# Stick-breaking attention: the softplus tile split in two on VectorE, its product with the triangle of minus ones in two reduced passes

## What is computed

```python
def stick_breaking(q, k, v):
    def block(args):
        q_blk, b_idx = args
        z = jnp.einsum('bqhd,bkhd->bhqk', q_blk, k).astype(jnp.float32) * scale
        q_pos = b_idx * SB_BLOCK + jnp.arange(SB_BLOCK)
        mask = key_pos[None, :] < q_pos[:, None]
        log_1mb = jnp.where(mask, jax.nn.log_sigmoid(-z), 0.0)
        after = lax.cumsum(log_1mb, axis=3, reverse=True) - log_1mb
        w = jnp.where(mask, jnp.exp(jax.nn.log_sigmoid(z) + after), 0.0)
        return jnp.einsum('bhqk,bkhd->bqhd', w.astype(v.dtype), v)
```

## Time and profile before

| | before |
|---|---|
| median of 3 runs | 3941.0 us |
| the 3 runs | 3942.57, 3941.0, 3927.64 us |
| span of the profiled execution | 3942.1 us (its time is not listed apart from the runs; the nearest run is 3942.57) |
| TensorE busy over the span | 93% |
| VectorE, ScalarE, GpSimd busy | 51%, 42%, 3% |
| stick-breaking stage, from the first L1342 to the last L1325 | 422.4 to 569.8 us, 147 us |

### The profile page before, as it was taken

One profiled execution on the slowest core, in us unless ns is written; L12 is line 12 of the kernel. 1 busy time (PEld: TensorE's weight loads), 2 busy tenths in 40 slices (PEclk: granted clock), 3 DMA queues, 4 the chain that ended last, 5 costly groups with the idle time before them and its releaser, 6 DMA issues. The chain is left out here.

```text
span 3942.1 us, 48364 instructions
## 1 busy us (share of the span) xinstructions
PE 3658.2 (93%) x18930; PEld 2963.7 (75%) x18930; DVE 2019.1 (51%) x3935; ACT 1663.9 (42%) x3110; POOL 107.9 (3%) x119
## 2 busy tenths in 40 slices
PE   7999889999997999999897999999879999999799
PEld 6888558778876777777776777777768788888686
DVE  3144442453345777776335455555555456666542
ACT  3222561444442444443125444444433466665420
POOL 0011220000000000000000000000000000000000
PEclk9999999989997889899999999999979999999799
DMA  4343412113222212122311110011132121110311
GB/s 143 115 134 105 141 45 89 54 64 107 96 72 83 57 44 54 51 57 65 123 43 58 28 33 28 28 28 30 35 108 75 49 65 43 38 38 17 137 61 43
DMA packets 219274, 264.57 MB, mean 67 GB/s; under 512 B 62636, under 2 KB 142628, under 8 KB 218024
## 3 DMA queue, kind: packets, MB, share of 16 engines
q1 hardware_dynamic: 219048, 261.48, 20.4%
HBM read 191.43 MB, written 69.99 MB: 66 GB/s over the span
## 5 line engine op out<-in xcount | busy, mean ns | idle before, releaser
L329 PE MATMUL bank<-wh,XH 128*128 128x512 f32 x1344 | 553.5, 412 | 23.3 <-DVE wl L313 18.2
L329 PE MATMUL bank<-wh,XL 128*128 128x512 f32 x1344 | 528.4, 393 | 0.0
L329 PE MATMUL bank<-wl,XH 128*128 128x512 f32 x1344 | 528.4, 393 | 0.0
L2600 PE MATMUL bank<-XH,wh 128*128 128x512 f32 x1040 | 426.2, 410 | 27.7 <-DVE wl L2589 26.1
L2600 PE MATMUL bank<-XH,wl 128*128 128x512 f32 x1040 | 410.5, 395 | 0.0
L2600 PE MATMUL bank<-XL,wh 128*128 128x512 f32 x1040 | 409.7, 394 | 0.0
L329 PEld LDWEIGHTS bank<-wh,XH 128*128 128x128 f32 x1344 | 255.8, 190 | 86.2 <-issue 18.2
L329 PEld LDWEIGHTS bank<-wh,XL 128*128 128x128 f32 x1344 | 256.0, 190 | 60.1 <-issue 10.0
L329 PEld LDWEIGHTS bank<-wl,XH 128*128 128x128 f32 x1344 | 255.4, 190 | 55.5
L329 PE MATMUL bank<-XH,wh 128*128 128x512 f32 x704 | 281.4, 400 | 7.9 <-DVE XL L1552 7.9
L313 DVE TENSOR_TENSOR wl<-raw,wh 128x1024 fp32r<-128x1024 f32 x128 | 157.3, 1239 | 250.6 <-ACT wh L304 249.3
(11 more groups left out here) (412 smaller groups left out, 7043.9 us busy)
## 6 DMA issues: line engine op xcount, KB each, us to landing
sc_zt<-stage SPq DMA_DIRECT2D x88, 256.0 KB, 2.0
raw<-in_att_w_in SPq DMA_DIRECT2D x33, 512.0 KB, 4.2
raw<-in_even_w_in SPq DMA_DIRECT2D x32, 512.0 KB, 5.3
raw<-in_odd_w_in SPq DMA_DIRECT2D x32, 512.0 KB, 4.7
raw<-in_rec_w_in SPq DMA_DIRECT2D x32, 512.0 KB, 4.0
sc_h<-H SPq DMA_DIRECT2D x24, 512.0 KB, 2.6
sc_z<-stage SPq DMA_DIRECT2D x40, 256.0 KB, 2.0
z<-sc_z SPq DMA_DIRECT2D x8, 1024.0 KB, 5.5
```

Of the source, the lines that this page charges most:

```text
L329: done = e.matmul(out, lhsT, rhs, start=k == 0 and j == 0, stop=k == NK - 1 and j == 2)
L2600: done = e.matmul(bank[:, :], x[:, k, :], y[:, k, ts], start=k == 0 and j == 0, stop=k == NK - 1 and j == 2)
```

## The change

The softplus tile is split on VectorE in two float32r tiles: `sph`, a cast of `sp` (which rounds it), and `spr`, the rest `sp` minus `sph`. The triangle gets a float32r copy `tri`, made once (minus one is exact in it). TensorE's product with the triangle becomes two float32r matmuls, tri times sph and tri times spr, in place of the full-precision one. The product with `nones`, the products for z and with v, and GpSimd's add (which still reads `sp`) stay.

```diff
+        self.tri = c.right("tri", [P, P], R32)
+        self.sph, self.spr = (c.sbs(n, [P, 512], 4, R32) for n in ("sph", "spr"))
...
             elif what == "sum":
-                e.wait_ge(*self.plus.at(h, half, kb))
-                e.matmul(bank[:, 0:n], self.ntri[:, :], self.spl[h][:, 0:n], start=False, stop=False, skip_group_check=True)
+                if kb == 7 and h == 0:
+                    e.wait_ge(*self.whole.at())
+                e.wait_ge(*self.rest.at(h, half, kb))
+                for s in (self.sph, self.spr):
+                    e.matmul(bank[:, 0:n], self.tri[:, :], s[h][:, 0:n], start=False, stop=False, skip_group_check=True)
...
         e.wait_ge(*self.tables.at("after"))
+        e.tensor_copy(self.tri[:, :], self.ntri[:, :]).then_inc(*self.whole.up())
...
                 done.then_inc(*self.plus.up(h, half, kb))
+                e.wait_ge(*self.plus.at(h, half, kb))
+                e.tensor_copy(self.sph[h][:, 0:n], s[:, 0:n]).then_inc(*self.halved.up(h, half, kb))
+                e.wait_ge(*self.halved.at(h, half, kb))
+                e.tensor_tensor(self.spr[h][:, 0:n], s[:, 0:n], f32(self.sph[h][:, 0:n]), ALU.subtract) \
+                    .then_inc(*self.rest.up(h, half, kb))
...
-    nc = _bacc.Bacc("TRN2", target_bir_lowering=False, num_devices=1)
+    nc = _bacc.Bacc("TRN2", target_bir_lowering=False, num_devices=1, dynamic_dma_scratch_size=1024)
```

More of the change, by code:

```diff
@@ L1276, in __init__ @@
         self.run = c.flag("po")
+        self.whole, self.halved, self.rest = (c.flag("ve") for _ in range(3))
         self.marks = [[(self.kepl, (h,)) for h in range(4)] + [(self.low, (h, s // 4)) for h in range(4)] for s in range(NS)]
```

## The result

The changed kernel takes 3957.39 us in the median of 14 runs, the kernel before 3941.09 us in the median of 14. The ratio is 1.0034, 95% interval 1.0022 to 1.0046, so 9 to 18 us slower (the two medians by themselves are 16.3 us apart, inside that interval). The forecast was 3941 with a range to 3950. The half per cent that was named as the bound of a difference isn't reached, but the time is outside the range, and the change is a loss. The stage, too, is outside what the prediction allowed ("longer by over 6" was its sign of being wrong).

The account below looks back on a forecast made before the run. TensorE was taken to bound the wide slots, waits the others. Gains of 6.4 us (wide slots) and 1.2 (last sums) cancelled against added waits and switches, sum 0.0: 3941 us, own range 3936 to 3946, with rivals 3927 to 3950.

Parts of the forecast that it names:

- longer by over 6: Sign of being wrong: the changed stage, forecast at 147 us within 5, comes out more than 6 us longer.
- The price of a pass and the wide slots: Full-width triangle product 0.46 us for 0.86; 16 wide slots hide VectorE's new work and win 6.4 us.
- switches between kinds of product: TensorE changing between full-precision and float32r matmuls: 0.04 us for each of 24 full-width products, +1 us.
- The mechanism in the masked slots: New VectorE work delays the mask of w that TensorE's weigh awaits: +2.0 (384 columns), +1.1 and +0.4 us (slots 4-7, 0-3).
- The loop of two slots: Masked slots: new work, mask of w and weigh set two slots' minimum length, 5.2 us with 384 columns.
- the sum above has no term for it: Port shared by VectorE and GpSimd: in wide slots the add ends at 3.7 us, when the cast begins; no cost.
- Rival 2: Shared port takes the wide slots' gain too: 3944 to 3947 us, 3950 with masked slots worse; chance 0.17.
- The cover of 2 us: Wide slots: split ends at 4.9 us, the triangle product needing it stands at 6.9 us, so VectorE's work is hidden.
- Where half 1 is mixed: Closed chain through masks, gate product and ScalarE: 0.57 us of 128-column split in each of four slots, +2.3 us.
- The last four sums: End of the stage: no begin beside them, TensorE is the bound again, a gain of 1.2 us.
- The ceiling: Gain if TensorE were the bound everywhere in the stage: 14.4 us, 0.37% of the time.
- Rival 3: Granted TensorE clock stays at 1.2 GHz through slots 4 to 11 and 36 to 43: +23 us, 3964 us; chance 0.04.

Follow-up runs that it names:

- e4_noadd: Changed kernel with GpSimd's running sum cut to one column of each item; stage 150.9 us, ratio to the kernel before 1.0014.
- e8_order_noadd: Changed kernel with the split moved behind the mask of w and GpSimd's running sum cut to one column; stage 139.3 us, ratio to before 0.9989.
- e6_kept: Changed kernel with the four retention splits moved from slots 12, 15, 18, 21 to wide slots 22, 24, 26, 28; stage 157.2 us, ratio 1.0028.
- e11_end: Changed kernel with the split at its slot's end, behind gate product and XL, and retention splits in wide slots; stage 140.8 us, ratio to before 0.9981.
- e12_halves: Changed kernel with the split at its slot's end and retention splits in 512-column halves within slots 18 to 28; stage 139.2 us, ratio to before 0.9983.
- e2_passes: Changed kernel without the split: softplus written as float32r once and read by both passes; stage 137.0 us, ratio to the kernel before 0.9974.
- e1_order: Changed kernel with cast and subtraction moved behind the mask of w of the item two slots older; stage 146.6 us, ratio to before 1.0002.
- e5_noadd_before: Kernel before the change with GpSimd's running sum cut to one column; stage 145.7 us, one run of 3951.43 us.

## Why the prediction was wrong

- **The price of a pass and the wide slots: right.** 0.46 for 0.86 us, slots of 3.03, casts of 0.43 and subtractions of 0.69 when undisturbed. The +1.0 for switches between kinds of product came to nothing.
- **The mechanism in the masked slots: right, its size wrong. This is the step that failed.** "This is the wait that I expect to take the gain's place" is the one that came. But slots 0 to 11 and 40 to 43 were put at +4.3 us (+3.5 for this term and +0.8 for the start), 12 to 15 at 0 and 16 to 19 at a gain of 1.6; measured +9.3, +3.1 and +3.1, 12.8 us more in all. The loop of two slots was laid out with undisturbed durations. With GpSimd's add out of the way (e4_noadd) the same three are +5.4, +1.2 and -0.4, so 9.3 of the 12.8 us are the port's. How the other 3.5 divide between kept (below) and a loop that was laid out a little too short isn't shown.
- **The port should have had a term; "the sum above has no term for it".** It was put at nothing in every slot. I checked the shared port in the wide slots only, where the add is indeed over when the cast begins (498.67 and 498.71 us in a steady one). In the masked slots and behind kept the add falls on the cast, the subtraction or the mask, and each meeting holds one of them up for the rest of the other. e4_noadd prices it at 11.5 us, e8_order_noadd at 7.3 even with the better place. Rival 2 had the mechanism, but in the wide slots, where it shows in one slot of 3.78 behind kept alone, and with 0.17.
- **Kept was not counted.** Slots 12, 15, 18 and 21 have 1.9 us more on VectorE. The cover of 2 us was worked out without it, and in slots 12 to 19 the masks take VectorE's room too. e6_kept wins 6.5 us there.
- **Where half 1 is mixed:** +2.3 forecast for slots 32 to 39, +3.7 measured, of which +2.6 are in slots 32 to 35. The other +1.1 are in 36 to 39, which have 256 columns like slots 4 to 7 and were left out of the sum. e11_end, which takes the split out of the chain, brings the eight slots to 20.2 us, and e12_halves, with the same order, to 21.2.
- **The last four sums:** a gain of 1.2 forecast, +1.1 measured; with the better place 1.9 were won there (15.8 for 17.7).
- **The ceiling was never the gain to be had.** With nothing added on VectorE it is 9.2 us of stage (e2_passes): the wide slots win their 0.40 each, the masked ones less, and in slots 12 to 15 the port takes some.
- **Rival 3, the clock,** has a part that no run isolates. By slots, the granted clock was 0.86 in 8 to 11 and 0.90 in 16 to 19, where it was 1.00, and 0.51 in 36 to 39, where it was 0.72. With the better place (e1_order) it is 1.00 in the first two groups, where the waits are gone, but 0.89 in 12 to 15, where two long slots are left, and 0.50 in 36 to 39. What the lower clock costs in these groups isn't known.
- **The chances:** 0.94 on within half a per cent was borne out, but the range of 3927 to 3950 held no case in which place, port and kept add up, though each was named or visible. The loss was 16 us against a bound of 20, so this chance came true although the sum behind it was wrong.

## What to carry to other kernels

Before adding work to an in-order queue, list what is queued behind the new instructions and who waits for it: with the same two instructions ahead of a mask that TensorE waits for the stage was 16.2 us longer than before, with them behind it 0.4. Where GpSimd's adds run beside VectorE instructions of the kinds that were stretched here (casts, subtractions of two tiles, masks), price each meeting, in every kind of slot and not in the regular one alone. And take the saving at what the slots that the engine really bounds can give.

## What the runs showed that was not expected

The records of VectorE and GpSimd instructions that meet are long, not late: a mask of 0.28 us shows 1.09 us, a subtraction of 1.23 us shows 2.17. So busy time rises by waiting. VectorE's added 53 us in the page are more than the split's own work, which is 44.0 us by the undisturbed groups of e4_noadd (cast and subtraction in four widths). The instruction that makes `sp` from the bank and `l` was not stretched: it has a mean of 0.69 us at 512 columns with the add and without. In the kernel before, the add lengthened the masks of `sp` (a mean of 0.33 us for 0.29), those of w (0.31 for 0.29) and kept's casts (0.85 for 0.68), and cost nothing that shows (e5_noadd_before, 0.5 us).
